# The last stage of a hybrid attention layer joined to the stage before it: one program without a barrier, a last turn with code of its own, and two steps of each chunk moved

## The reference, cut to what matters

```python
h   = rmsnorm(x) * (1 + scale) + shift                 # from the conditioning vector
qa, ka, va, za, qb, kb, vb, zb, ga, gb = h @ w_in      # one projection, split by columns
oa  = neighbourhood_attention(qa, ka, va, cache_a)     # branch A, 8 heads x 64
ob  = window_attention_with_sink(qb, kb, vb, cache_b)  # branch B, 8 query heads, 2 kv heads
ya  = (oa * silu(za)) @ w_br_a                         # 512 -> 1024
yb  = (ob * silu(zb)) @ w_br_b
m   = sigmoid(ga) * ya + sigmoid(gb) * yb
y   = rmsnorm(x + gate * (m @ w_out)) * final_gain
```

## Time and profile before

| | |
|---|---|
| median of 3 runs | 1318.19 us (1318.03 to 1318.77) |
| the profiled execution | 1318.47 us |
| its span, first to last instruction | 1316.7 us |
| TensorE busy in the span | 1226.8 us (93%) |
| mean granted clock of TensorE | 0.983 of full speed |

### The profile page before, as it was taken

The page is one execution under the profiler, slowest core; times in us unless marked ns, Lnnn a source line. Parts: engine busy times, 40 slices in busy tenths (PEclk is TensorE's granted clock), DMA queues, the critical chain, the costliest instruction groups (busy, mean ns, idle before and its releaser), DMA issues. The chain is left out here.

```text
span 1316.7 us, 23695 instructions
## 1 busy us (share of the span) xinstructions
PE 1226.8 (93%) x7888; PEld 1115.1 (85%) x7888; DVE 832.3 (63%) x1668; ACT 610.2 (46%) x1233; POOL 202.0 (15%) x211
## 2 busy tenths in 40 slices
PE   7999899999999999998999999999989767999997
PEld 1699789988998998898889889889989766988886
DVE  2468458747746775775687688588588464444342
ACT  3432235525543563464465466456456453432341
POOL 0000023104302310330000000000000046333430
PEclk9999999999999999999999999999999988999999
DMA  9346532233123213324212310411411187434440
GB/s 364 118 177 208 187 107 73 69 112 105 60 101 112 72 48 129 113 72 127 93 53 54 95 52 31 128 52 36 128 47 36 59 289 241 145 126 151 153 160 32
DMA packets 87396, 148.63 MB, mean 113 GB/s; under 512 B 7574, under 2 KB 65430, under 8 KB 87324
## 3 DMA queue, kind: packets, MB, share of 16 engines
q1 hardware_dynamic: 70764, 125.69, 29.5%
q10 hardware_dynamic: 16560, 22.15, 4.7%
HBM read 112.42 MB, written 35.40 MB: 112 GB/s over the span
## 5 line engine op out<-in xcount | busy, mean ns | idle before, releaser
L83 PE MATMUL d_ps_pairs<-h,wt 128*128 128x320 f32 x2304 | 359.4, 311 | 0.0
L83 PEld LDWEIGHTS d_ps_pairs<-h,wt 128*128 128x128 f32 x2304 | 338.9, 188 | 0.3
L1261 DVE TENSOR_TENSOR pt<-t_ps_pairs,pt 128x512 fp32r<-128x512 f32 (+1 forms) x272 | 158.3, 621 | 38.4 <-ACT pt L1074 37.1
L1085 ACT ACTIVATE pr<-s_ps_pairs,mx 128x896 f32<-128x896 f32 (+1 forms) x160 | 143.1, 897 | 83.5 <-DVE mx L1304 44.8
L83 PE MATMUL s_ps_pairs<-h,wt 128*128 128x512 f32 (+1 forms) x864 | 170.9, 359 | 8.4 <-DVE wt L1327 4.9
L83 PEld LDWEIGHTS s_ps_pairs<-h,wt 128*128 128x128 f32 x864 | 144.5, 193 | 31.1 <-DVE wt L1327 5.1
L1074 ACT ACTIVATE pt<-t_ps_pairs 128x512 fp32r<-128x512 f32 (+1 forms) x272 | 135.2, 547 | 38.4 <-PE t_ps_pairs L949 32.3
L949 PE MATMUL t_ps_pairs<-ident_sb,pr 128*128 128x128 f32 x960 | 133.6, 277 | 15.6 <-DVE pr L1320 7.7
L83 PE MATMUL b_ps<-og_f,wb_f 128*128 128x256 f32 x960 | 120.0, 287 | 25.0 <-DVE wb_f L1662 15.9
L83 PEld LDWEIGHTS b_ps<-og_f,wb_f 128*128 128x128 f32 x960 | 118.2, 195 | 27.0 <-DVE wb_f L1662 17.1
L949 PEld LDWEIGHTS t_ps_pairs<-ident_sb,pr 128*128 128x128 f32 x960 | 109.2, 141 | 25.2 <-DVE pt L1261 13.3
(11 more groups left out here) (159 smaller groups left out, 1653.2 us busy)
## 6 DMA issues: line engine op xcount, KB each, us to landing
gates_d<-gst ACTq DMA_DIRECT2D x96, 160.0 KB, 1.8
wraw<-in_w_gate SPq DMA_DIRECT2D x25, 512.0 KB, 3.4
gt_f<-gates_d SPq DMA_DIRECT2D x40, 256.0 KB, 4.2
comb_a<-in_bias SPq DMA_DIRECT2D x24, 384.0 KB, 3.4
vw_a<-v_d SPq DMA_DIRECT2D x64, 128.0 KB
v_d<-vst SPq DMA_DIRECT2D x20, 320.0 KB, 4.5
wada<-in_w_ada SPq DMA_DIRECT2D x12, 512.0 KB, 5.5
kk<-kb_d SPq DMA_DIRECT2D x16, 320.0 KB, 5.9
```

Of the source, the lines that this page charges most:

```text
L83: mm = eng.matmul(out, lhs(a, k), rhs(b, k), start=(k == 0 and i == 0), stop=(k == n_k - 1 and i == 2))
L1085: act.activation(probs_run(s, t), scores_run(s, t), ACT.Exp, bias=mx[:, t:t + 1], scale=-1.0, accum_out=den[:, t:t + 1]).then_inc(exp_done, 1)
L1261: dve.tensor_tensor(pt[:, 1, c * 512:c * 512 + cols], t_ps[:, n % 2, 0:cols], pt[:, 0, c * 512:c * 512 + cols].bitcast(F32), ALU.subtract) ...
```

## The change

- **One block.** `build` opens one block for all stages. All SBUF and PSUM places are laid out beforehand, and tiles of the last stage lie over tiles of `pairs`. Instead of the barrier, each first use waits for the last use of what it covers. Weight tiles 0 and 1 lie in `wt`. Tiles 2 to 7 of `w_br` and the first four of `w_out` lie over `hm`.
- **The last pair of branch B** is written out behind a loop of three turns (`turns` in `pairs`, `last=True`). In it `load_tile` loads w_br tiles 0 and 1 in place of the tiles of zeros, and the second of them is split at step 8 instead of the end of the turn. The first 256 tokens of `ost` are stored after step 6. ACT takes the SiLU of the four pieces of the first chunk after steps 9 and 10. DVE makes product, high part and low part of the pieces (`first_gated`): one within step 10, three after it. Then come the splits of tiles 2 and 3.
- **The last stage** stages its weight tiles in `craw`, the halves of `x`, and `wraw`. Tiles 2 to 5, the four pieces and two of the gates are loaded within the last pair. Tile 6 waits for the split of tile 2. SP then waits until the last store of `o_d` has landed before it goes on with tile 7. The first chunk takes (j, branch) in plain order, where before (1, 0) stood ahead of (0, 1).
- **Between chunks** ACT takes the first two sigmoids of the next chunk before the square and root of the second half (`root(i - 1, 1)`), and DVE scales that half after the products of j = 0 (`scaled(i - 1, 1)`).

```diff
@@ pairs
+    def turns(eng, body):
+        with eng.Fori(0, PAIRS if A else PAIRS - 1) as p:
+            body(p, False)
+        if not A:
+            body(PAIRS - 1, True)
@@ pairs, sync
-                if i >= PROJ:
+                if last and ahead:
+                    src = io["w_br"][n // 2]
+                elif i >= PROJ:
@@ pairs, scalar
             def tile_highs(s):
                 for n, (_, _, at) in enumerate(SPLITS):
-                    if at == s:
+                    if (LAST_AT if last and n == 3 else at) == s:
                         tile_high(n)
...
                 if s < STEPS:
                     tile_highs(s)
+                if last and s == 6:
+                    act.wait_ge(o_done, pb * STEPS + 4)
+                    act.dma_start(io["o_d"][pb, :, 0:2 * P], ost[:, 0:2 * P]).then_inc(o_out, 16)
+                if last and s >= STEPS - 1:
+                    first_silu(act, f, 2 * (s - STEPS + 1))
+                    first_silu(act, f, 2 * (s - STEPS + 1) + 1)
             gate(STEPS + 1)
             gate_out(STEPS + 1)
-            tile_highs(STEPS)
+            if not last:
+                tile_highs(STEPS)
+            if last:
+                act.wait_ge(d_done, (pb + 1) * GPP * UNITS)
+                tile_high_f(act, f, 2)
+                tile_high_f(act, f, 3)
...
-        if not A:
-            act.wait_ge(g_out[0], 2 * PAIRS * GPP * UNITS // 2 * 16)
-            act.wait_ge(g_out[1], 2 * PAIRS * GPP * UNITS // 2 * 16)
-            act.wait_ge(o_out, PAIRS * O_STORES * 16)
-            act.wait_ge(ko_out_a, PAIRS * 16)
@@ pairs, vector
                 if s == STEPS:
                     add_halves(s - 2)
+                    if last:
+                        first_gated(dve, f, 0)
...
+            if last:
+                for n in range(1, 4):
+                    first_gated(dve, f, n)
+                tile_low_f(dve, f, 2)
             add_halves(STEPS - 1)
-            tile_lows(STEPS)
+            if not last:
+                tile_lows(STEPS)
@@ new
+def first_gated(dve, f, n):
+    oz0, og = f["oz0"], f["og"]
+    dve.wait_ge(f["silu_done"], n + 1)
+    dve.tensor_tensor(oz0[:, n, 1, :, :], oz0[:, n, 1, :, :], oz0[:, n, 0, :, :], ALU.mult).then_inc(f["og_prod"], 1)
+    dve.wait_ge(f["og_prod"], n + 1)
+    dve.tensor_copy(og[:, n, 0, :, :], oz0[:, n, 1, :, :]).then_inc(f["og_hi"], 1)
+    dve.wait_ge(f["og_hi"], n + 1)
+    dve.tensor_tensor(og[:, n, 1, :, :], oz0[:, n, 1, :, :], og[:, n, 0, :, :].bitcast(F32), ALU.subtract
+                      ).then_inc(f["og_lo"], 1)
@@ finish
-        block = ctx.enter_context(nc.Block())
-        EXTRA = [[3], [4, 5], [6], [7, 8], [9], [10, 11], [12], [13, 14], [15]]
+    EXTRA = [[4], [5, 6], [7], [8, 9], [10], [11, 12], [13], [14, 15]]
@@ finish, sync
+        sp.wait_ge(o_out_a, PAIRS * 16)
+        sp.wait_ge(g_out[0], PAIRS * HALF * 16)
+        sp.wait_ge(g_out[1], PAIRS * HALF * 16)
+        sp.wait_ge(x_used, PAIRS * 3)
+        for n in range(PIECES):
+            if n == 2:
+                sp.wait_ge(o_out, (PAIRS - 1) * 32 + 16)
+            ... (two DMAs into oz0[:, n])
+        sp.wait_ge(c_split, 3 * ALL)
+        load_w(2)
+        sp.wait_ge(s_done, ALL * STEPS)
+        load_w(3)
+        load_w(4)
+        sp.wait_ge(w_lo, TILES_TOTAL)
+        load_w(5)
+        sp.wait_ge(m_done, ALL * 2 * STEPS)
+        sp.wait_ge(g_out[0], (ALL - 1) * HALF * 16)
+        sp.wait_ge(g_out[1], (ALL - 1) * HALF * 16)
+        load_gt(0, 0)
+        load_gt(0, 1)
+        sp.wait_ge(pvb_done, ALL * (STEPS - 2))
+        load_gt(0, 2)
+        load_gt(0, 3)
+        load_w(6)
+        sp.wait_ge(g_out[0], ALL * HALF * 16)
+        sp.wait_ge(g_out[1], ALL * HALF * 16)
+        sp.wait_ge(o_out, PAIRS * 32 + 16)
@@ finish, scalar
+            sigmoid(i, 0)
+            sigmoid(i, 1)
+            if not first:
+                root(i - 1, 1, isinstance(i, int) and i == 1)
+            for j in range(KD):
+                if 0 < j < KD - 1:
+                    sigmoid(i, j + 1)
...
+            root(i, 0, first)
+            if last:
+                root(i, 1, first)
@@ finish, tensor
-                work = [(j, br) for j in range(KD) for br in range(2)]
-                if first:
-                    work[0:4] = [(0, 0), (1, 0), (0, 1), (1, 1)]
+            for j in range(KD):
+                for br in range(2):
@@ finish, vector
+        tile_low_f(dve, f, 3)
...
+                if j == 0 and not first:
+                    scaled(i - 1, 1)
...
+                if e == 0 or last:
+                    scaled(i, e)
```

More of the change, by code:

```diff
@@ L633, in _, with pairs @@
         value(19)
[L635 removed]
+    return [(v_out[i], 16 * 2 * TT // 4) for i in range(4)] + [(out_done, 192)], v_lo
 SWAP16 = [(i + 16) % 32 for i in range(32)]
[L641 removed]
+def pairs(nc, io, block, hm, ident, wt, wraw, craw, w_in, w_hi, w_lo, tiles, own, counts, earlier_stage, branch, f=None):
     A = branch == "a"
[L650 to L651 removed]
     def sem(name):
@@ L772, in _, with body @@
             sp.dma_start(sin[:, :], io["sin"]).then_inc(const_in, 16)
-        with sp.Fori(0, PAIRS) as p:
+        def body(p, last):
             pb = p + base
@@ L840, in _ @@
                 load_tile(4)
+        turns(sp, body)
     @block.gpsimd
@@ L873, in _, with body @@
         pe.wait_ge(w_lo, BEFORE)
-        with pe.Fori(0, PAIRS) as p:
+        def body(p, last):
             pb = p + base
@@ L1018, in _, with body @@
             act.dma_start(band[:, :, :], io["band"]).then_inc(band_in, 16)
-        with act.Fori(0, PAIRS) as p:
+        def body(p, last):
             pb = p + base
@@ L1106, in tile_high @@
             def tile_high(n):
-                i = SPLITS[n][0]
+                i = SPLITS[n][0] if not (last and n == 3) else 2
                 act.wait_ge(w_in, (p * TILES + BEFORE + n + 1) * 16)
@@ L1183, in _, with body @@
             dve.wait_ge(nsk_done, 1)
-        with dve.Fori(0, PAIRS) as p:
+        def body(p, last):
             pb = p + base
@@ new lines, in body, with weight, weight_raw, wait_split @@
+            if not last:
+                tile_lows(STEPS)
+        turns(dve, body)
+    return o_out, (ko_out if A else x_used)
+CT = 256
+PIECES = 4
+GSLOTS = 4
+CHUNKS_ = TOK // CT
+WT = 2 * KD
+DVE_TILES = [m for m in range(2, WT) if m < KD or m % 2 == 0]
+POOL_TILES = [m for m in range(2, WT) if m not in DVE_TILES]
+def weight(f, m, part):
+    return f["wb"][m][:, part, :] if m < KD else f["wo"][m - KD][:, part, :]
+def weight_raw(f, m):
+    return f["stage"][(m - 2) % 4]
+def wait_split(eng, f, m):
+    if m in DVE_TILES:
+        eng.wait_ge(f["w_lo_dve"], DVE_TILES.index(m) + 1)
+    elif m in POOL_TILES:
+        eng.wait_ge(f["w_lo_pool"], POOL_TILES.index(m) + 1)
@@ new lines, in build @@
+    counts = {n: nc.alloc_semaphore(name=n + "_pairs") for n in COUNTS + ("g_out0", "g_out1", "sink_in")}
+    f = finish_tables(nc, own_f)
+    with nc.Block() as block:
+        stored, v_lo = front(nc, io, block, left, right, later, ident, small["scol"], hm, wv, wkb, wt, wraw, craw,
+                             w_in, w_hi, w_lo)
+        o_out_a, ko_out = pairs(nc, io, block, hm, ident, wt, wraw, craw, w_in, w_hi, w_lo, tiles, own_a, counts,
+                                (stored, v_lo), "a")
+        o_out, x_used = pairs(nc, io, block, hm, ident, wt, wraw, craw, w_in, w_hi, w_lo, tiles, own_b, counts,
+                              (o_out_a, ko_out), "b", f)
+        finish(nc, io, block, f, counts, w_lo, o_out_a, ko_out, o_out, x_used)
```

616 lines of the change are left out of this document (298 added, 318 removed).

## The result

The changed kernel takes 1298.67 us (median of 4 runs, 1297.56 to 1301.35), the kernel before 1318.48 (4 runs, 1318.03 to 1322.05): ratio 0.9847, 95% interval 0.9824 to 0.987. That is 19.8 us less; forecast were 24.5 (1293.7 us, range 1287 to 1303). The profiled execution took 1298.77 us, its span is 1296.9, its mean granted clock 0.990 (before 0.983).

A forecast was written before the change was run, and what follows sets the result against it. TensorE, busy 93% of the span, was taken to bound the kernel. First chunk's end 1104.1 plus four chunks 180.5 is 1284.6; tail 7.6 gives span 1292.2; 1.8 outside it, less 0.3, gives 1293.7 us, range 1287 to 1303.

The forecast's parts named there:

- Start of the last stage: Between last pair and last stage: without the barrier TensorE starts at 1045.4, where a 15.9 us gap stood before.
- Last pair, cost 0: Last pair of branch B: added SiLUs, pieces and moved tile split stay hidden; cost 0, upper bound 0.5 us.
- First half of the first chunk: Last stage's first 192 matmuls: 23.2 us plus 2.9 us of stalls, for four pieces and for `tp`.
- Weight stream: First chunk's second half: POOL's rounds of 4.4 us delay tiles 11, 13 and 15; TensorE loses 8.5 us, bounds 6 to 12.
- Clock: First chunk: TensorE's clock falls after sparse work and costs 2.2 us as before, bounds 0 to 3.
- Boundaries: Four chunk boundaries: sigmoids ahead of the square remove TensorE's waits for `tp`; gain 5.7 us, lower bound 3.
- a wait at j = 3: Sign in the profile after: such a TensorE wait in a later chunk would show the boundary was worked out wrong.
- a drain of about 1380 ns: Table loads at chunk boundaries: if present, four boundaries would each lose about 1 us again, 1298 instead of 1294.
- Four later chunks: Chunks after the first: they took 186.2 us, lose 5.7 us of boundary waits, and so take 180.5.

The follow-up runs named there:

- own_code: Kernel before, with only the last pair of branch B written out after the loop on every engine: 1325.16 us, ratio 1.0021.
- lows_dve: Changed kernel with the low parts of weight tiles 9, 11, 13 and 15 made on DVE instead of POOL: 1293.3 us, ratio 0.9791.
- mg_64: Changed kernel with `mg` and the tiles behind it moved to start at a multiple of 64 bytes: 1298.21 us, ratio 0.9823.
- again: Changed kernel timed once more, unedited, beside the other runs: 1299.15 us, ratio 0.9838.
- store_later: Changed kernel with SP's waits for the last stores moved behind the loads of weight tiles 7 and 8: 1299.43 us, ratio 0.9829.
- before_wo_pairs: Kernel before, with high and low halves of each w_out tile 4 KB apart instead of 32 KB: 1322.18 us, ratio 1.0006.
- wo_halves: Changed kernel with `mg` at a multiple of 64 bytes and w_out halves 16 KB and 12 KB apart: 1297.78 us, ratio 0.9821.
- before_mg_32: Kernel before, with `mg` alone moved 32 bytes off a multiple of 64: 1322.68 us, ratio 1.0009.
- no_boundary: Changed kernel with the root and scaling of a chunk's second half back in their old places: 1306.68 us, ratio 0.9894.

## Why the prediction came out as it did

The sign, the range and the mechanism held. The point was 5 us too low. Span against span, 1296.9 against 1292.2, each step by the rows after:

- *Start of the last stage*: forecast 1045.4, measured 1047.0, +1.6. That is no cost of the pair. Where the pair starts, after is already 1.8 us behind before; over the pair this shrinks by 0.3. In the traces of the twelve experiments the pair starts between 2.1 us earlier and 4.4 later than in the profiled execution of before, 2.5 in the middle: 2.0, 4.2 and 3.7 later in the three edits of before, 2.1 earlier to 4.4 later in the nine edits of after. So the traces show no difference between the two kernels here, and the base was off: the one profiled execution, and the three runs beside it, lay at the low end of what the kernel before does. 51 more runs of it have medians of 1320.8 to 1321.0.
- *Last pair, cost 0*: right. The split at step 8 and the pieces are hidden. `own_code` gives -0.3 for the pair, too. TensorE's first `b_ps` comes at once.
- *First half of the first chunk*: forecast 26.1 us with 2.9 of stalls, measured 27.1 (1046.84 to 1073.91), +1.0. The wait before (0, 1) is 1.28 where I had 1.9. The `tp` that j = 2 needs starts at 1053.70, is there at 1054.1 (forecast 1053.3) and isn't waited for. Two waits that the sum had at 0.5 in all are 0.88 and 0.95: ahead of the `tp` that they wait for, DVE makes the low halves of tiles 5, 6 and 10, in 1.73, 1.77 and 1.81 us where one takes 1.23 elsewhere. The waits in brackets come to 3.1, only 0.2 above the forecast. Most of the other 0.8 is what a wait costs beyond its brackets: by the start times of the matmuls the three waits delay TensorE by 3.6 us, and two smaller delays of 0.1 us each come on top. Between them the matmuls keep their 0.120 us.
- *Weight stream*: forecast 8.5 us lost at tiles 11, 13 and 15, measured 2.09 + 2.60 + 0.15 + 3.21 = 8.05. They are ready at 1078.1, 1082.4 and 1087.6, against 1075.8, 1080.3 and 1084.7; 1.6 of that is the later start, 0.7 was lost by tile 11, and for tile 15 another 0.6 in the rounds behind it. The mechanism is the one named (POOL's sum, ACT's copy, low part of `mg`, tile):

```profile
1075.76 2.35 POOL L1667 TENSOR_TENSOR wo<-x_f,wo 128x1024 fp32r<-128x1024 f32 x1
1078.08 0.72 POOL L1675 TENSOR_TENSOR tp<-tp 128x256 f32<-128x256 f32 x1
1079.33 0.74 POOL L1678 TENSOR_TENSOR mg<-tp,mg 128x256 fp32r<-128x256 f32 x1 [0.53 <-ACT mg L1646]
1080.02 2.34 POOL L1667 TENSOR_TENSOR wo<-wraw,wo 128x1024 fp32r<-128x1024 f32 x1
1082.32 1.71 POOL L1675 TENSOR_TENSOR tp<-tp 128x256 f32<-128x256 f32 x1
...
1085.24 2.34 POOL L1667 TENSOR_TENSOR wo<-x_f,wo 128x1024 fp32r<-128x1024 f32 x1
```

  The first round is 4.26 us, the next 5.22, since the sum behind it took 1.71 in place of 0.74. `lows_dve` takes the rounds away and wins 5.9 us. Note what this means for the sum: the end of the first chunk hangs on tile 15, 2.9 us late, and with it comes the chunk's end, 2.8 us late (1106.9 for 1104.1). The waits of the first half don't add to that. In `mg_64` one of them is 0.8 us longer (1.73 for 0.95), and the wait for tile 11 is 1.0 shorter (1.08 for 2.09).
- *Clock*: forecast 2.2 us in the first 24 `y_ps` matmuls; the stretches above show one fall, and the whole half (32.99 us, less 8.05 of waits and 22.5 of matmuls) leaves 2.4 for it and for what the matmuls lose besides. The last 75 matmuls, in which the fall lies, take 19.34 us instead of 75/96 of 22.65 = 17.7: 1.6 of it is the clock. About right.
- *Boundaries*: forecast a gain of 5.7 and no wait. Right in this trace, and on the low side: taken back alone they cost 7.5 us, since a wait there can also drop the clock. The rows of after that answer to the earlier trace rows:

```profile
1151.22 1.28 ACT L1620 ACT_TABLE_LOAD   x1
...
1152.52 1.16 ACT L1620 ACTIVATE gt<-gt 128x512 f32<-128x512 f32 x2
1152.64 0.68 DVE L1777 TENSOR_TENSOR y_f<-y_ps,gate_f 128x512 f32<-128x512 f32 x1
...
1155.39 0.78 DVE L1756 TENSOR_TENSOR tp<-b_ps,gt 128x256 f32<-128x256 f32 x2
1155.41 1.06 ACT L1625 ACTIVATE x_f<-y_f 128x1024 f32<-128x1024 f32 x1 [1.73 <-DVE y_f L1779]
...
1158.40 1.28 DVE L1744 SCALAR_TENSOR_TENSOR y_f<-y_f,norm_f,gain_f 128x1024 f32<-128x1024 f32 x1
...
1159.60 1.27 DVE L1756 TENSOR_TENSOR tp<-b_ps,gt 128x256 f32<-128x256 f32 x3
```

  With T = 1152.68 `tp` starts at T + 2.7 and again at T + 6.9, and the first product of each is there 0.43 us later: T + 3.1 and T + 7.3, each 1.0 us sooner than I had worked out (4.1 and 8.4). DVE's work on the second half starts at T itself, where before it started at T + 0.9. TensorE comes to j = 3 at T + 8.6, so the spare time there was 1.3 us, not 0.4.

  That holds for the last three boundaries. At the first (T = 1106.90) the two `tp` are there at T + 4.4 and T + 8.7, which is just when TensorE wants the second. There DVE's work on the first half of the chunk stands behind the gating of the next chunk's pieces, and ACT waits for the DMA of these:

```profile
1096.59 0.63 ACT L1615 ACTIVATE oz<-oz 128x512 f32<-128x512 f32 x1 [8.60 <-DMA oz<-gates_d]
```

  DVE comes to the chunk's first half at 1100.71, at T - 6.2, in the later chunks at T - 7.3 to T - 7.5. So the first boundary has nothing to spare, and other traces of the same schedule show a wait there: 0.42 us at j = 3 in `again`, 0.39 in `mg_64`, 1.9 in all in `store_later`. The prediction had named a wait at j = 3 as the sign of a boundary read wrong. For the first boundary that sign is there: the prediction worked out all four from rows of the second.

  In the row above the sigmoids begin 0.02 us behind the table load here too. The Trainium skill (ScalarE: Activation LUTs, "What ACT_TABLE_LOAD costs") adds a drain of about 1380 ns to each load. With it the prediction's estimate was 1298, near where the kernel did come out, but not for that reason: no such drain stands in the rows.
- *Four later chunks*: forecast 180.5 us, measured 1289.3 - 1106.9 = 182.4, +1.9. Here failed "Those took 1309.1 - 1122.9 = 186.2 and lose 5.7: 180.5": it took the pace of the `y_ps` matmuls as given. They take 0.70 us more in each chunk, 2.8 in four and some 0.6 in the first. (The boundaries gave 0.9 more than forecast, which hides a part.) The change re-laid the last stage's tiles in SBUF, and the prediction said nothing of what that could cost.

1.6 + 1.0 + 0.4 (second half of the first chunk) + 1.9 is 4.9; the spans differ by 4.7. This adds up by place. By cause it is the base (1.6), POOL's later rounds (1.3), and the pace of the `y_ps` matmuls, less what the boundaries gave.

Of the pace, 0.17 of the 0.70 us hangs on where `mg` and the tiles behind it start. For the other 0.5 the distance of the w_out halves and the written-out pair are ruled out (`own_code` has 21.95). The addresses of w_out are unlikely, since `before_wo_pairs` and `wo_halves` change nearly all of them and keep the pace, and `y_ps` lies at the same place in PSUM in both built programs. What stays is the address of `mg` itself, which differs in both kernels even where both are multiples of 64, the places of the other tiles, and the order of the program around the loop. Nothing here tells these apart, so the cause of this part stays open.

## What to carry to other kernels

Where a stage is joined to the one before, work out which engine's round paces the first operands of the new stage. Here one line that gave POOL's share to DVE was worth 5.9 us beside the change's 20. Write the layout of SBUF down as a part of the change and compare the time of one uninterrupted group of matmuls before and after. Where a wait at a joint has hidden something, expect it to come to light when the wait goes: the slower matmuls cost nothing in `before_mg_32` and their full price after the change. And take a base from more runs than the profiled one: 1.6 of 5 us of error came from that.

## What the hardware did that I had not expected

The start times of single matmuls show how the pace of `y_ps` depends on places. With full clock and no wait they come 227, 227, 226 ns apart in the kernel before, and in `before_wo_pairs` and `own_code`. With `mg` 32 bytes off, alternately 235 and 232 ns. In the kernel after, a pattern of seven repeats (234, 231, 238, 237, 231, 234, 235 ns), and with `mg` on a multiple of 64 another (228, 230, 233, 241, 232, 231, 232 ns), which is the same in `wo_halves`. The shapes, types and order of these matmuls are the same in all. The `b_ps` matmuls are not slowed: they come 120 ns apart on the average in both kernels, and 192 of them take 23.0 us after the change (1152.68 to 1175.70). In `mg_64`, where `og` has moved with `mg`, it is 118.7 ns in the last three chunks.

A wait of 2.63 us at the first boundary of `no_boundary` was followed by a clock of 0.50, and one of 2.00 in `own_code` by 0.57. Waits of 0.87 to 1.07 at the later boundaries of `no_boundary`, and of up to 1.91 in before, were not.
